# Expert weight chunks loaded as two transfers of 64 partitions instead of one of 128

## What is computed

```python
capacity = CAPACITY_FACTOR * t // N_EXPERTS            # 2 * 256 // 16 = 32
gate, idx = lax.top_k(jnp.swapaxes(affinity, 1, 2), capacity)
xe = jax.vmap(lambda hb, ib: hb[ib])(h, idx)
hidden = jax.nn.silu(einsum('becd,edf->becf', xe, w_gate)) * einsum('becd,edf->becf', xe, w_up)
ye = einsum('becf,efd->becd', hidden, w_down) * gate[..., None]
```

## Time and profile before

| | |
|---|---|
| median of 3 runs | 1473.33 us (1472.71 to 1473.81) |
| the profiled execution | 1473.55 us, span 1471.8 us |
| TensorE busy | 1129.7 us (77% of the span) |
| VectorE, ScalarE busy | 468.1 us, 374.7 us |
| granted TensorE clock, mean | 0.892 of full speed |
| bytes from HBM | 491.52 MB |
| DMA queue of SyncE | 492.07 MB, its packets took 82.4% of the 16 DMA engines' span |

### The profile page before, as it was taken

How to read it: one execution, slowest core, us unless ns; L and a number is a source line. 1 busy time by engine, 2 the same in 40 slices (tenths; PEclk the granted TensorE clock), 3 DMA queues, 4 the chain that set the end, 5 groups by cost and what they waited for, 6 DMA issues and landing times.

```text
span 1471.8 us, 20240 instructions
## 1 busy us (share of the span) xinstructions
PE 1129.7 (77%) x8437; PEld 684.3 (46%) x8437; DVE 468.1 (32%) x879; ACT 374.7 (25%) x623; POOL 49.0 (3%) x107
## 2 busy tenths in 40 slices
PE   9999999965656566656656657566566999999998
PEld 8887887521212212212112122122121688999887
DVE  6988885100000000000000000000000478675546
ACT  6658663100001001001001000000100465465434
POOL 1220120000000000000000000000000020000000
PEclk9999999997878968888798687886887999999999
DMA  8663528999999999999999999999999764555551
GB/s 307 200 245 108 206 87 370 420 426 427 427 426 430 428 428 427 427 429 427 426 430 428 427 427 427 428 428 427 430 427 428 294 186 172 172 184 189 196 186 47
DMA packets 58922, 493.33 MB, mean 335 GB/s; under 512 B 6715, under 2 KB 8309, under 8 KB 34165
## 3 DMA queue, kind: packets, MB, share of 16 engines
q1 hardware_dynamic: 58724, 492.07, 82.4%
q10 hardware_dynamic: 144, 0.52, 0.1%
HBM read 491.52 MB, written 1.05 MB: 335 GB/s over the span
## 4 chain that ended last, share of the span: by engine, by line
DMA 54%; PE 40%; DVE 3%; ACT 1%; issue 1%; SPq 0%; ACTq 0%; DVEq 0%
DMA arena<-in_expert_w_down 19%; DMA arena<-in_expert_w_up 18%; DMA arena<-in_expert_w_gate 17%; PE ps L1927 13%; PE ps L2020 7%; PE ps L1932 7%; PE ps L2374 4%; PE ps L2398 2%; PE ps L1999 1%; PE ps L2190 1%; PE ps L2221 1%; DVE w_split L1199 1%; PE ps L1897 1%; PE ps L2134 1%; PE ps L2109 1%
## 5 line engine op out<-in xcount | busy, mean ns | idle before, releaser
L2374 PE MATMUL ps<-ring,arena 128*32 128x512 f32 x1024 | 168.3, 793 | 115.5 <-DMA ring<-in_expert_w_up 60.1
L2374 PE MATMUL ps<-arena 128*32 128x512 f32 x1024 | 163.2, 772 | 115.4 <-DMA arena<-in_expert_w_up 58.6
L1199 DVE TENSOR_TENSOR w_split<-ring,w_split 128x1024 fp32r<-128x1024 f32 (+3 forms) x178 | 201.9, 1141 | 93.6 <-ACT w_split L765 92.3
L765 ACT ACTIVATE w_split<-ring 128x1024 fp32r<-128x1024 f32 (+3 forms) x178 | 175.2, 991 | 180.5 <-PE ps L1932 126.8
L1651 DVE TENSOR_TENSOR arena<-arena,ps 128x512 f32<-128x512 f32 x16 | 11.0, 688 | 557.8 <-PE ps L2374 557.8
L2374 PEld LDWEIGHTS ps<-ring,arena 128*32 128x32 f32 x1024 | 32.9, 127 | 241.5 <-DMA ring<-in_expert_w_up 101.1
L2374 PEld LDWEIGHTS ps<-arena 128*32 128x32 f32 x1024 | 32.7, 126 | 236.0 <-DMA arena<-in_expert_w_up 96.1
L2020 PE MATMUL ps<-hT_hi,w_split 128*128 128x256 f32 x608 | 111.8, 284 | 0.5 <-ACT w_split L765 0.4
L2398 PE MATMUL ps<-arena 128*32 128x256 f32 x1072 | 81.2, 455 | 32.9 <-DMA arena<-in_expert_w_down 27.8
L2398 PE MATMUL ps<-ring,arena 128*32 128x256 f32 x896 | 69.9, 465 | 43.1 <-DMA ring<-in_expert_w_down 40.1
L2020 PEld LDWEIGHTS ps<-hT_hi,w_split 128*128 128x128 f32 x608 | 95.3, 192 | 2.3 <-issue 1.0
(11 more groups left out here) (360 smaller groups left out, 1379.0 us busy)
## 6 DMA issues: line engine op xcount, KB each, us to landing
ring<-in_expert_w_up SPq DMA_DIRECT2D x36, 2048.0 KB, 36.2
arena<-in_expert_w_gate SPq DMA_DIRECT2D x35, 2048.0 KB, 35.6
ring<-in_expert_w_gate SPq DMA_DIRECT2D x28, 2048.0 KB, 35.9
arena<-in_expert_w_up SPq DMA_DIRECT2D x28, 2048.0 KB, 37.2
arena<-in_expert_w_down SPq DMA_DIRECT2D x25, 2048.0 KB, 37.1
ring<-in_expert_w_down SPq DMA_DIRECT2D x21, 2048.0 KB, 37.1
ring<-in_w_ff SPq DMA_DIRECT2D x32, 1024.0 KB, 5.0
ring<-in_w_in SPq DMA_DIRECT2D x23, 1024.0 KB, 5.0
```

What stands on the lines that cost most here:

```text
L765: act.activation(w_split[:, n % WBUFS, 0, 0:cols], slot_view(slot, cols)[:, n % 2, :], ACT.Copy).then_inc(split_hi, 1)
L1199: dve.tensor_tensor(buf[:, 1, :], w, buf[:, 0, :].bitcast(F32), ALU.subtract).then_inc(split_lo, 1)
L2374: m = pe.matmul(ps[j * CAP:(j + 1) * CAP, bank, :], xe[:, kt, :], w[r][:, j * FCOL:(j + 1) * FCOL], start=kt == 0, stop=kt == KT - 1, skip ...
```

## The change

`load_chunk` issues, for each chunk, one transfer for partitions 0 to 63 and one for 64 to 127, directly behind each other on the same queue and with the same semaphore; each row is still one run of 16 KB (12 KB in an expert's last chunk). The pieces that stay at 128 partitions are the last 4 KB of each expert's last chunk (`TAIL:WIDE`), the chunk `HALVED`, and the first half of chunk 12. The semaphore counts that TensorE waits for double accordingly. Nothing else is changed.

```diff
         def landed_count(n):
 
             if n < SLOTS:
-                return 32 if n == HALVED else 16
-            return 16 * ((n - SLOTS) // TURNING + 2)
+                return 32
+            return 32 * ((n - SLOTS) // TURNING + 2)
...
             def load_chunk(slot, loaded, e, k):
 
+                source = chunk_source(e, k)
+                words = WIDE if k < EXPERT_CHUNKS - 1 else TAIL
+                for rows in (slice(0, P // 2), slice(P // 2, P)):
+                    sp.dma_start(slot[rows, 0:words], source[rows, 0:words]).then_inc(loaded, 16)
                 if k < EXPERT_CHUNKS - 1:
-                    sp.dma_start(slot, chunk_source(e, k)).then_inc(loaded, 16)
                     return
-                source = chunk_source(e, k)
-                sp.dma_start(slot[:, 0:TAIL], source[:, 0:TAIL]).then_inc(loaded, 16)
                 sp.dma_start(slot[:, TAIL:WIDE], source[:, TAIL:WIDE]).then_inc(tail_loaded, 16)
...
                     sp.wait_ge(chunk_used, slot_free(n))
-                    sp.dma_start(slot[:, WIDE // 2:WIDE], source[:, WIDE // 2:WIDE]).then_inc(loaded, 16)
+                    for rows in (slice(0, P // 2), slice(P // 2, P)):
+                        sp.dma_start(slot[rows, WIDE // 2:WIDE], source[rows, WIDE // 2:WIDE]).then_inc(loaded, 16)
...
-                        pe.wait_ge(slot_loaded[turn(n)], 16 * (PAIR * EXPERT_CHUNKS // TURNING) * pair_i +
-                                   16 * ((n - SLOTS) // TURNING + 2))
+                        pe.wait_ge(slot_loaded[turn(n)], 32 * (PAIR * EXPERT_CHUNKS // TURNING) * pair_i +
+                                   32 * ((n - SLOTS) // TURNING + 2))
```

## The result

The changed kernel takes 2337.27 us (median of 4 runs, 2329.34 to 2359.21) against 1473.02 us before: ratio 1.589, 95% interval 1.585 to 1.592. The forecast was 2371 us. The profiled execution is the longest of the four, 2359.21 us with a span of 2357.3. The four differ by 1.3%; what follows compares with the median, and where a kernel had two executions of which one was over 1.5% longer, with the shorter.

The account below looks back on a forecast made before the run. The prediction took the expert stage's DMA stream as the bound, 188 chunks of 4.90 us without cover. Sum: 1473.55 + 896 (182.75 cut chunks, each 4.90 us longer) + 2 = 2371 us, range 1560 to 2400 us.

Parts of the forecast that it names:

- What bounds the kernel: Expert stage from 224 us: 188 chunk steps of 4.90 us on the DMA engines, TensorE waiting, no cover: 921 us.
- The issues and the ends of transfers: SyncE's one more issue per chunk costs nothing; one more transfer end in each queue costs 0 to 15 us.
- Where the bytes go: Rate to 64 partitions in the expert stage: cut chunk between 4.90 and 9.80 us; upper bound taken, +896 us.
- the likeliest case: Expert stage at doubled steps, engines sharing entrances: 2320 to 2400 us, low end 9.53 us per chunk; chance 0.64.
- The whole-width pieces: `HALVED`, half of chunk 12 and last quarters of 15 experts' last chunks keep their rate; 182.75 of 188 chunks pay.
- Small terms: Before 224 us: 0 to 5 us; last two chunks' matmuls at the slow clock level: +2 us, bound 0 to 8.
- Rival A: Engines in the expert stage spread out half a chunk apart, neither is slowed: 1560 to 2280 us; chance 0.17.
- Rivals B and C: No shared entrance in expert stage; transfer ends cost: B 1474 to 1489 us (chance 0.11), C about 1474 (0.05).
- Rival D: Engines alternating between two sides fill each other's pauses, stream up to 440 GB/s: 25 us less, 1449 us; chance 0.03.

Follow-up runs that it names:

- run 1: Against the changed kernel, each chunk is two transfers cut by columns, each to all 128 partitions in 8 KB runs: 1487.92 us, 1.009 of the kernel before.
- Runs 5 and 6: Changed kernel with halves reading every second row over the whole 2 MB: 2353.25 us; with halves reading one contiguous MB but writing all 128 partitions: 1485.93 us.
- run 4: Changed kernel with the first half of chunk 12 written as eight transfers of 8 partitions and one of 64: 2316.54 us, 2397.97 in a second execution.
- run 7: Changed kernel with only the first two experts' 24 chunks cut, the 168 of the loop whole-width: 1561.56 us, ratio 1.060 to the kernel before.
- run 8: Changed kernel with only one chunk in four cut by partitions, eight chunks in flight: 2132.83 us, 2178.52 in a second execution.
- run 2: Changed kernel with each chunk as three transfers, partitions 32 to 95, 0 to 31 and 96 to 127: 2226.52 us, ratio 1.51 to the kernel before.
- run 9: Changed kernel with one chunk in four cut and at most three chunks in flight in the loop instead of eight: 1863.03 us.
- run 10: Changed kernel with every second chunk cut and at most three chunks in flight in the loop instead of eight: 2310.83 us.

## Why the prediction was right

*What bounds the kernel.* Right: 188 steps without cover, from 224 us on. The spans differ by what the expert stage took more, and the second layer begins 885.4 us later.

*The issues and the ends of transfers.* Costed at nothing, with bounds 0 and 15 us. In a whole-width stream 187 more of them, in runs of half the length, cost 13.7 us (run 1), near the upper bound. But its shorter packets alone account for that, and the change keeps the long ones, so the 0.08 us of the earlier trace rows is not confirmed, and nothing speaks against the average over eight experts in the earlier trace rows. In the changed kernel itself that term can't be told apart. SyncE's issues became slower (line L529 has a median of 0.54 us and at worst 6.3 us for `w_up` into `ring`, against 0.33 in the earlier trace rows), and it cost nothing, since landings are 70 us behind.

*Where the bytes go.* The upper bound was the right one, and the forecast's size was off in one term: a cut chunk takes 9.62 us, not 9.80. 182.75 x (9.62 - 4.90) = 863 us instead of 896, and 1473 + 863 + 2 = 2338 us, where the median is 2337. The 9.80 us came from entrances to the memory that two engines share. That was a supposition: no run shows such entrances or the sharing; what the runs show is the step of 9.62 us. If each two engines do share one, they move 218 GB/s / 8 = 27.3 GB/s together, a little more than one moves in the kernel before (428 / 16 = 26.7), as the low end of the likeliest case had it (9.53 us). Runs 5 and 6 exclude HBM as the place, run 1 the transfers' number and size. What is shown is that a stream of transfers that write 64 partitions each, low and high in turn, runs at half the rate, 218 against 428 GB/s.

*The whole-width pieces.* The sum let 5.25 chunks keep their rate. In the profiled execution the last quarter of an expert's last chunk did not: from 1217.83 to 1237.36 are 19.53 us for two chunks, where 1.75 cut ones and a quarter whole one would take 18.06. That is 1.47 us for each of 15 experts, 22 us, the distance of this execution (2359) from the median (2337). The 4 KB packets of these quarters agree: their median between 640 and 1107 us is 319 ns, against 159 in the kernel before. Whether the three shorter executions were spared it, their times suggest and no trace of them shows.

*Small terms.* The pieces after the last chunk's landing were slow as feared: 3.69 and 1.84 us for the last L2400 and L2407 pieces, against 1.91 and 1.14 in the earlier trace rows, 2.5 us where 2 were put.

*Rival A* brought no time: the rate is 217 to 219 GB/s in every slice of the stage's middle. The engines keep their distance to each other: in the seven chunks that land from 1150.59 to 1208.33 us the adds of the first half come at the same places behind the first one, to 0.05 us. But they are not level: the last comes 4.5 us behind the first, in a step of 4.81 us for half a chunk, where it had been 2.2 us at 292 us. They have spread out, as rival A had it, without any gain, and run 4 put two groups of eight half a chunk apart with no gain either. So the upper bound was the right choice, but it was an estimate of mine, and that engines half a chunk apart would be free of each other is not borne out as far as the runs go; to that extent the forecast was lucky. Which engines would share an entrance, no trace says. *Rivals B and C* are what run 1 does (421 GB/s), whose transfers write all partitions. *Rival D*: no slice of any page is above 430 GB/s.

*What stays open.* Theory 1 in its simple form, two engines that share one entrance and all others free, was not shown; it gives the time of the changed kernel and of run 7 to within 2 us (with 9.62 us for a cut chunk), and nearly the packets of run 8 while the engines are level. It gives neither the mixtures afterwards nor, if the shift parted the engines that share, run 4. The other reading, that a transfer to 64 partitions is slow whichever they are and whatever the other engines write, fits the change, run 7 and run 4 as well, but not the fast packets at the start of run 2. The test that would part them was not made: a stream of 64-partition transfers that each take rows from both halves, such as every second partition. Why a whole-width transfer is slowed by engines that are in a cut one, and the more so the further the engines stand apart, is open too.

## What to carry to other kernels

Write all 128 partitions with each transfer of a stream that is bound by the DMA engines; if a load must be in pieces, cut it by columns (here 0.9%) and not by partitions (here 59%). DMA share at 1.0 did not mean here that the engines moved what they can (1.01 at 428 and at 218 GB/s): read the GB/s beside it. A few narrow transfers in such a stream cost more here than their own bytes (one chunk in four cut: 660 us where 215 were additive), since the whole-width ones near them were slow too; keep them together (run 7, 4.86 us each), or keep the queue short around them if they are few (run 9, 270 us less than run 8; with every second chunk cut, run 10, it gained nothing).

## What the runs showed that was not expected

- One chunk in four cut costs 660 us where four times that share costs 864: 76% of the loss for 25% of the cuts.
- Three chunks in flight are enough for the whole-width stream: 1472.72 us against 1473.22 with eight.
- The kernels with cut chunks scatter more: 2329 to 2359 us after the change and 2317 to 2398 us in run 4, where the kernel before keeps within about 2 us. Why was not looked into.
- The DMA engines did not work the deep queue level with each other. In run 8 the first engine is through with a chunk 42 to 61 us before the last (medians of 640 to 1107 and 1107 to 1500 us).
